# A constant matrix multiplied into an unread bank in TensorE's waits between routing and the first expert

## The chip, the cores and the metric

One NeuronCore of a Trainium2 chip runs the whole program. The metric is device time in microseconds (us) of one execution, lower is better. The time before is given as the median of three runs.

## What is computed

One decoder layer over 512 tokens of width 1024, all in float32. In the reference, cut to what matters here:

```python
h2 = rmsnorm(x, norm_ffn[i])
x = x + hierarchical_moe(h2, w_coarse[i], w_fine[i], w_expert_up[i], w_expert_down[i])

def hierarchical_moe(h, w_coarse, w_fine, w_up, w_down):
    coarse = jax.nn.softmax((t @ w_coarse).astype(f32), axis=-1)
    g_prob, g_idx = lax.top_k(coarse, 1)               # 1 of 4 groups
    ...
    top_vals, top_idx = lax.top_k(fine, TOP_K)         # 2 of its 4 experts
    top_w = jax.nn.softmax(top_vals, axis=-1) * g_prob
    ...
    gu = jnp.einsum('nd,edf->nef', t, w_up)
    act = jax.nn.silu(g_part) * u_part * gates[..., None].astype(t.dtype)
    out = jnp.einsum('nef,efd->nd', act, w_down)
```

Ahead of this stand a first RMSNorm, one input projection, a state-space branch and sliding-window attention side by side, gates that merge them, and an output projection that is added to x. There are 16 experts; each token goes to two of them.

## The kernel before

Every engine has its own program, written out by hand; semaphores tie them together. On each engine instructions run in the order written, so an instruction that waits holds up all behind it. Nothing plans the order: it is the text of the five blocks (`block.sync` for weight loads, `block.gpsimd` for gathers and scatters, `block.scalar`, `block.vector`, `block.tensor`).

Precision. Most large products take float32 operands that are split into a high part (rounded by a ScalarE copy into an fp32r tile) and a low part (VectorE subtracts the high part). TensorE then makes three fp32r products: high by high, high by low, low by high. So each weight piece costs ScalarE one pass and VectorE one pass before TensorE can use it. `product` (L1758 to L1764) does this for the first half of the kernel (lines L1761 to L1763), `up` (L2138 to L2140) for the experts' first matrix, `down_` (L2185 to L2192) for the second.

Beginning. TensorE waits for the tile of ones, which GpSimd writes (`ones_ready`, L610), and for the row of norm gains, which a DMA brings. Two matmuls (L1746) with one row of ones spread that row over 128 partitions in the banks `mb[0]` and `mb[1]`. VectorE multiplies the normalised rows by them (`scale_tile`, L1098). TensorE turns each tile of 128 tokens (`turn_tile`, L1755), ScalarE copies the high part (`turned_high`), VectorE takes the low part (L1152), and TensorE makes the keys and values of the tile (`keys_values`) into the banks `pj[0]` and `pj[1]` in turn. At the same time SyncE issues the loads of the first weight pieces and of many small parameters.

Output projection and routing. The output projection goes over eight units (two halves of the columns by four tiles of 128 tokens). Behind each unit TensorE turns its result (`turn_rows2`, L2010) and multiplies it by the router's weights (`router`, L2019) into `sc[0]`. When the last unit is done, the program goes on in this order:

1. VectorE ranks the logits in some fifteen small instructions and writes `chosen` (L1582).
2. TensorE multiplies `chosen` by a triangular matrix and by ones, to count the place of each token in its expert's list (L2075, L2078), and counts the tokens of each expert (L2081, into `mb[0]`).
3. VectorE writes `pos` (L1594) and, for each expert, a matrix `pick` that is one where a token has a given place (`pick_list`, L1603).
4. TensorE multiplies `pick` by the token numbers: `place_index` (L2090) for experts 0 and 1. VectorE makes them indices (L1624), and GpSimd's indirect DMA gathers the rows of that expert (L681) from `h2_rows` in memory, which `act.dma_start` (L973) has stored tile by tile.
5. VectorE computes each token's shares (L1628 to L1637) from an exponential that ScalarE makes (L1049), behind its two high parts of the first expert's weights (L982). TensorE places them (`place_shares`, L2098).
6. VectorE takes the low part of the first half of the first expert's weights (`low_up`, L1618) and the picks of experts 2 and 3.
7. TensorE turns the gathered rows (`turn_rows`, L2124), ScalarE and VectorE split them (`high_rows` L988, `low_rows` L1652, tile `xt_low`), and TensorE places lists 2 and 3 (`place_lists`, L2111).

Experts. For each expert e TensorE runs `up(e)` over eight slices of 128 (24 matmuls, waiting for each half of the weights, `up_low_done`, and of the rows, `xt_done`), the next two lists, the transposes of the activations of expert e-1 (`turn_act`), the transposes of the rows of expert e+1, and `down_(e-1)` into `mb[0]` and `mb[1]`. VectorE for expert e reads lists, makes two picks, takes the low parts of the two halves of expert e+1 (L1618) with the low part of a second matrix between them (L1672), of the activations (L1676) and of the rows (L1652), and then the product of gate and value (`swiglu`, L1658, L1660). Loads of weight halves go into a ring of 12 places, each released by `half_used` of TensorE.

Of the banks, `mb[1]` is last read before the output projection and next written by `down_(0)`; `pj[1]` is first written by the keys and values of the second tile. Each of these next writes starts an accumulation group anew.

The lines that set the order around the change:

```python
            pe.wait_ge(r_pe, 1)
            pe.wait_ge(const_ready, 8)
            pe.matmul(sc[0][:, 0:TT * NE], before[:], chosen[:].rearrange("p t e -> p (t e)"), start=True, stop=False)
...
            pe.wait_ge(route_done, 1)
...
            for e in range(2):
                place_index(e)
            place_shares()
            turn_rows(0)
            pe.wait_ge(idx_done, 1)
            place_lists(LISTS[1], LISTS[2])
            for e in range(NE - 1):
                up(e, range(DC))
```

Of the kernel before, what the change touches and what calls it, by code (L numbers as in the profile page):

```python
# [14 lines left out]
P = 128  # L15
# [9 lines left out]
def hybrid_layer(nc, x, norm_mix, w_in, lam_re, lam_im, log_dt, b_re, b_im, c_re, c_im, d_skip,  # L25
# [35 lines left out]
    with ExitStack() as ctx:  # L61
        def sb(name, shape, dt=F32):
            return ctx.enter_context(nc.sbuf_tensor(name, shape, dt))
# [121 lines left out]
        ones = sb("ones", [P, P], F32R)  # L185
# [51 lines left out]
        def bank(name):  # L237
            return ctx.enter_context(nc.psum_tensor(name, [P, 512], F32))

        pj = [bank("pj0"), bank("pj1")]  # L240
        tp = [bank("tp0"), bank("tp1")]
        sc_both, mb_both = (ctx.enter_context(nc.psum_tensor(name, [P, 2, 512], F32)) for name in ("sc_both", "m_both"))
        sc, mb = ([banks[:, b, :] for b in range(2)] for banks in (sc_both, mb_both))
# [134 lines left out]
        def out_bank(u, i):  # L378

            if u in BY_PIECE:  # L380
                return pj[i][:, 0:256]
            return pj[(u + 1) % 2][:, i * 256:(i + 1) * 256]

        def turned_bank(u, i):

            if u == BY_PIECE[1]:
                return tp[(u + i) % 2][:, 0:2 * P]
            return tp[u % 2][:, 2 * P * i:2 * P * (i + 1)]
# [47 lines left out]
        def expert(e):  # L436

            return e % NG * EPG + e // NG
# [20 lines left out]
        def piece_w(n, /, **dims):  # L459
            z = piece_size(n)  # L460
            pat = "p (%s) -> p %s" % (" ".join(dims), " ".join(dims))
            return [w[split_place(n)][:, 0:z].rearrange(pat, **dims) for w in (w_high, w_low)]
# [1272 lines left out]
        def _(pe):  # L1735
# [4 lines left out]
                return b  # L1740

            pe.wait_ge(ones_ready, 1)
            pe.wait_ge(mix_gain_loaded, 16)
            for f in range(2):
                pe.matmul(mb[f][:], ones[0:1, :].bitcast(F32), mix_gain[:, f * 512:(f + 1) * 512], start=True, stop=True  # L1746
                          ).then_inc(gain_full, 1)

            def turn_tile(t):
                for f in range(2):  # L1750
                    pe.wait_ge(xn_done, 2 * t + f + 1)
                    if t >= 2:
                        pe.wait_ge(h_low_done, 2 * (t - 2) + f + 1)
                    for k in range(4):
                        ins = pe.transpose(h_bank(t, f)[:, k * P:(k + 1) * P], xn[:, t, (4 * f + k) * P:(4 * f + k + 1) * P], ident[:])  # L1755
                    ins.then_inc(h_full, 1)

            def product(dst, terms, first=True, last=True):  # L1758

                for i, ((sh, sl), (mh, ml)) in enumerate(terms):  # L1760
                    pe.matmul(dst, sh, mh, start=first and i == 0, stop=False)  # L1761
                    pe.matmul(dst, sh, ml, start=False, stop=False)  # L1762
                    ins = pe.matmul(dst, sl, mh, start=False, stop=last and i == len(terms) - 1)  # L1763
                return ins  # L1764
# [235 lines left out]
            def turn_rows2(u, i):  # L2000

                hf, t = UNITS[u]
                pe.wait_ge(x2_done, 2 * u + i + 1)
                if u < 2:
                    pe.wait_ge(tp_free[u], (n_tp + 1 - u) // 2)
                else:
                    pe.wait_ge(h2T_done, 2 * u if u == BY_PIECE[1] and i else 2 * (u - 1))
                for k in range(2):
                    c0 = hf * 512 + (2 * i + k) * P
                    ins = pe.transpose(turned_bank(u, i)[:, k * P:(k + 1) * P], x2[:, t, c0:c0 + P], ident[:])  # L2010
                ins.then_inc(tp_full, 1)

            def router(u):

                hf, t = UNITS[u]
                for k in range(4):
                    if k % 2 == 0:
                        pe.wait_ge(h2T_done, 2 * u + k // 2 + 1)
                    ins = pe.matmul(sc[0][:, t * (NG + NE):(t + 1) * (NG + NE)], x2T[u % 2][:, k, :], rw[:, 4 * hf + k, :],  # L2019
                                    start=u == 0 and k == 0, stop=hf == 1 and k == 3, skip_group_check=True)  # L2020
                ins.then_inc(lg_full, 1)

            def out_piece(u, i, ks):

                hf, t = UNITS[u]
                w = piece_w(P_OUT + 2 * hf + i, k=DC, n=256)
                tok = slice(t * P, (t + 1) * P)
                for k in ks:
                    if u == 0:
                        pe.wait_ge(m_low_done, k + 1)  # L2030
                    ins = product(out_bank(u, i), [(both(m_hl, k, tok), both(w, k, slice(None)))], k == 0, k == DC - 1)
                return ins
# [34 lines left out]
            out_piece(u, 1, first_k)  # L2067
            turn_rows2(u, 0)
            out_piece(u, 1, last_k).then_inc(pj_full, 1)
            turn_rows2(u, 1)  # L2070
            router(u)

            pe.wait_ge(r_pe, 1)
            pe.wait_ge(const_ready, 8)
            pe.matmul(sc[0][:, 0:TT * NE], before[:], chosen[:].rearrange("p t e -> p (t e)"), start=True, stop=False)  # L2075
# [5 lines left out]
                ins = pe.matmul(mb[0][:, 0:NE], ones[:], chosen[:, t, :], start=t == 0, stop=t == TT - 1)  # L2081
            ins.then_inc(lg_full, 1)

            pe.wait_ge(route_done, 1)

            def place_index(e):

                pe.wait_ge(pick_done, e + 1)
                for t in range(TT):
                    ins = pe.matmul(sc[e][:, 128:130], pick[e][:, t, :], tg[:, expert(e), t, 0:2], start=t == 0, stop=t == TT - 1)  # L2090
                ins.then_inc(idx_full, 1)

            def place_shares():

                pe.wait_ge(shares_done, 1)
                for e in range(2):
                    for t in range(TT):
                        ins = pe.matmul(sc[0][:, 132 + 2 * e:134 + 2 * e], pick[e][:, t, :], tg[:, expert(e), t, 2:4], start=t == 0, stop=t == TT - 1)  # L2098
                ins.then_inc(idx_full, 1)

            def place_lists(lo, hi):
                for e in range(lo, hi):
                    place_list(e)

            def place_list(e):

                k = sum(e >= lo for lo in LISTS[1:])
                c0 = list_at(k) + 4 * (e - LISTS[k])
                pe.wait_ge(pick_done, e + 1)
                for t in range(TT):  # L2110
                    ins = pe.matmul(sc[0][:, c0:c0 + 4], pick[e % 2][:, t, :], tg[:, expert(e), t, :], start=t == 0, stop=t == TT - 1)  # L2111
                ins.then_inc(idx_full, 1)

            def row_chunk(rows, k):

                return rows.rearrange("r (a p b) -> r a b p", p=P, b=2)[:, k // 2, k % 2, :]

            def turn_rows(e):
                pe.wait_ge(gathered[e % 2], 16 * (e // 2 + 1))
                for f in range(2):  # L2120
                    if e:
                        pe.wait_ge(xt_done, e * 2 + (f - 1))
                    for k in range(4):
                        ins = pe.transpose(tp[f][:, k * P:(k + 1) * P], row_chunk(xg[e % 2], 4 * f + k), ident[:])  # L2124
                    ins.then_inc(xt_full, 1)
# [44 lines left out]
            def turn_act(e):  # L2170
                pe.wait_ge(act_done, (e + 1) * 2)
                if e:
                    pe.wait_ge(at_done, 2 * e)
                    pe.wait_ge(at_low_done, e)
                for k in range(2):
                    ins = pe.transpose(sc[1][:, k * P:(k + 1) * P], act_e[e % 2][:, k * P:(k + 1) * P], ident[:])
                ins.then_inc(at_full, 1)
# [29 lines left out]

            for e in range(2):
                place_index(e)
            place_shares()  # L2210
            turn_rows(0)
            pe.wait_ge(idx_done, 1)
            place_lists(LISTS[1], LISTS[2])
            for e in range(NE - 1):
                up(e, range(DC))
                if e < LAST_LISTS:
                    pe.wait_ge(idx_done, e + 2)
                    place_lists(LISTS[e + 2], LISTS[e + 3])
                if e:
                    turn_act(e - 1)  # L2220
                turn_rows(e + 1)
                if e:
                    down_(e - 1)
# [69 lines left out]
```

## Time and profile before

| what | value |
|---|---|
| median of three runs | 528.2 us (527.18 to 528.49) |
| the profiled execution: its own time | 527.75 us |
| the profiled execution: its span | 526.0 us |
| mean granted TensorE clock | 0.978 |
| TensorE (PE) busy | 502.1 us, 95% |
| VectorE (DVE) busy | 389.2 us, 74% |
| ScalarE (ACT) busy | 295.0 us, 56% |
| GpSimd (POOL) busy | 130.3 us, 25% |
| memory traffic | 94.21 MB, mean 179 GB/s |

The profile shows one execution, from its first to its last instruction (the span); the execution's own time is 1.75 us longer. Times are microseconds from the start of the span. "L2138" is line 2138 of the kernel. An instruction row names the engine, the line, the operation and "tile written <- tiles read"; in brackets stands the idle time of the engine before it, and what ended it. A row with "x8" merges eight instructions.
### The profile page before, as it was taken

Reading aid. Unit: us, or ns where it says so; the run is one execution under the profiler, and the core shown is the slowest. Engines: PE = TensorE matmul, PEld = TensorE weight load, DVE = VectorE, ACT = ScalarE, POOL = GpSimd, SP = SyncE. Lnnn points to the kernel's source line nnn. Section 1 sums busy time; section 2 is a strip of 40 time slices with the busy share of each in tenths; the row PEclk is TensorE's granted clock in tenths of the full one; section 3 lists DMA queues with packets and bytes.
Section 4 is the critical chain, followed back from the end, with each engine's and each line's share of the span. In section 5 each row is a group of like instructions: output and inputs, shape, how many; then the busy total and the mean of one; then the engine's idle time right before and its main releaser. Section 6 shows DMA issues by size and latency. Waiting matters only on the chain.

```text
span 526.0 us, 7338 instructions
## 1 busy us (share of the span) xinstructions
PE 502.1 (95%) x2634; PEld 408.9 (78%) x2634; DVE 389.2 (74%) x609; ACT 295.0 (56%) x522; POOL 130.3 (25%) x185
## 2 busy tenths in 40 slices
PE   6999999999999999999999999779999999999994
PEld 4888788787877887778888888767887777777773
DVE  4889876999898768765758423578988878878851
ACT  6634144767867777632335102344767778778751
POOL 1229429294570000000000000032223232222221
PEclk9999999999999999999999999858999999999999
DMA  8560562022112220244678547569999999987432
GB/s 312 73 224 1 126 196 80 1 81 80 31 51 80 62 61 0 61 120 121 186 274 295 226 190 290 189 228 412 376 331 332 327 341 349 314 298 201 144 54 45
DMA packets 62343, 94.21 MB, mean 179 GB/s; under 512 B 13952, under 2 KB 45728, under 8 KB 62306
## 3 DMA queue, kind: packets, MB, share of 16 engines
q1 hardware_dynamic: 56304, 80.84, 45.2%
q0 software_dynamic: 4752, 8.67, 6.9%
q10 hardware_dynamic: 1250, 4.22, 2.0%
q8 instruction: 22, 0.36, 0.3%
q14 instruction: 15, 0.12, 0.1%
HBM read 88.72 MB, written 12.58 MB: 193 GB/s over the span
## 4 chain that ended last, share of the span: by engine, by line
PE 78%; DVE 10%; SPq 4%; ACT 3%; DMA 2%; issue 2%; POOL 0%; DVEq 0%; POOLq 0%; ACTq 0%
PE pj L1761 10%; PE pj L1763 10%; PE pj L1762 10%; PE pj L2138 5%; PE pj L2140 5%; PE pj L2139 5%; PE m_both L2185 5%; PE tp L2124 3%; SPq L521 2%; DVE split L433 1%; PE m_both L2190 1%; PE m_both L2192 1%; PE m_both L2191 1%; PE m_both L1761 1%; PE sc_both L1762 1%
## 5 line engine op out<-in xcount | busy, mean ns | idle before, releaser
L1761 PE MATMUL pj<-h_high,split 128*128 128x512 f32 x192 | 76.7, 399 | 0.0
L1763 PE MATMUL pj<-h_high,split 128*128 128x512 f32 x192 | 74.9, 390 | 0.0
L1762 PE MATMUL pj<-h_low,split 128*128 128x512 f32 x192 | 74.8, 390 | 0.0
L1618 DVE TENSOR_TENSOR up_low<-arena_front,up_high 128x2048 fp32r<-128x2048 f32 x23 | 52.7, 2290 | 11.4 <-ACT up_high L982 11.3
L622 POOL TENSOR_TENSOR rstd<-ssq,half_col 128x1 f32<-128x1 f32 x8 | 4.4, 555 | 194.3 <-DVE ssq L1116 181.4
L982 ACT ACTIVATE up_high<-arena_front 128x2048 fp32r<-128x2048 f32 x23 | 44.2, 1927 | 10.8 <-PE pj L2140 9.7
L2138 PE MATMUL pj<-up_high,xt_high 128*128 128x512 f32 x120 | 48.0, 400 | 0.9 <-DVE xt_low L1652 0.9
L2140 PE MATMUL pj<-up_high,xt_low 128*128 128x512 f32 x120 | 47.7, 397 | 0.0
L2139 PE MATMUL pj<-up_low,xt_high 128*128 128x512 f32 x120 | 47.6, 397 | 0.0
L433 DVE TENSOR_TENSOR split<-arena_front,split 128x2048 fp32r<-128x2048 f32 (+1 forms) x20 | 42.7, 2136 | 5.1 <-ACT split L414 5.1
L414 ACT ACTIVATE split<-arena_front 128x2048 fp32r<-128x2048 f32 (+1 forms) x20 | 34.8, 1742 | 17.9 <-PE sc_both L1763 10.9
L1761 PEld LDWEIGHTS pj<-h_high,split 128*128 128x128 f32 x192 | 36.1, 188 | 9.6 <-issue 2.3
L1763 PEld LDWEIGHTS pj<-h_high,split 128*128 128x128 f32 x192 | 36.0, 188 | 7.8
L1762 PEld LDWEIGHTS pj<-h_low,split 128*128 128x128 f32 x192 | 36.1, 188 | 6.9
L689 POOL DMA_INDIRECT out_dram<-arena_back,idx_all x15 | 25.9, 1729 | 61.6 <-ACT arena_back L1013 53.5
L681 POOL DMA_INDIRECT arena_front<-h_rows,idx_all x16 | 20.1, 1255 | 68.8 <-PE tp L2124 56.7
L2185 PE MATMUL m_both<-arena_back 128*128 128x512 f32 x60 | 28.2, 593 | 0.0
L2138 PEld LDWEIGHTS pj<-up_high,xt_high 128*128 128x128 f32 x120 | 23.2, 194 | 6.0 <-DVE xt_low L1652 1.1
L2139 PEld LDWEIGHTS pj<-up_low,xt_high 128*128 128x128 f32 x120 | 23.2, 193 | 4.9
L2140 PEld LDWEIGHTS pj<-up_high,xt_low 128*128 128x128 f32 x120 | 23.1, 192 | 5.0
L1013 ACT ACTIVATE arena_back<-m_both,gate_all 128x512 f32<-128x512 f32 x30 | 19.0, 686 | 12.9 <-PE m_both L2192 12.9
L962 ACT ACTIVATE arena_back<-arena_back 128x512 f32<-128x512 f32 x8 | 5.0, 630 | 36.8 <-DVE arena_back L1139 36.8
(340 smaller groups left out, 1283.0 us busy)
## 6 DMA issues: line engine op xcount, KB each, us to landing
arena_front<-in_w_expert_up_dram SPq DMA_DIRECT2D x23, 1024.0 KB, 11.6
arena_back<-in_w_expert_down_dram SPq DMA_DIRECT2D x16, 1024.0 KB, 12.7
arena_front<-in_w_in_dram SPq DMA_DIRECT2D x12, 1024.0 KB, 5.3
arena_back<-in_w_expert_up_dram SPq DMA_DIRECT2D x9, 1024.0 KB, 13.4
arena_front<-in_w_out_dram SPq DMA_DIRECT2D x4, 1024.0 KB, 6.0
arena_back<-in_x_dram SPq DMA_DIRECT2D x4, 512.0 KB, 6.2
arena_front<-in_w_ssm_glu_gate_dram SPq DMA_DIRECT2D x8, 256.0 KB, 2.7
arena_front<-in_w_ssm_glu_val_dram SPq DMA_DIRECT2D x8, 256.0 KB, 3.2
```

The source lines that it names most:

```text
L414: nc.scalar.activation(w_high[split_place(n)][:, 0:z], raw[n % 2][:, 0:z], ACT.Copy).then_inc(high_done, 1)
L433: eng.tensor_tensor(w_low[s][:, 0:z], raw[n % 2][:, 0:z], w_high[s][:, 0:z].bitcast(F32), ALU.subtract).then_inc(low_done, 1)
L689: g.indirect_dma_start(out_rows, bass.IndirectOffsetOnAxis(idx_all[:, e:e + 1], 0), y_out[e % 2], None, compute_op=ALU.add, bounds_check=S ...
L982: act.activation(up_high[i % 3][:], ring[i % NH], ACT.Copy).then_inc(up_high_done, 1)
L1618: tt(up_low[i % NH][:], ring[i % NH], up_high[i % 3][:].bitcast(F32), ALU.subtract).then_inc(up_low_done, 1)
L1761: pe.matmul(dst, sh, mh, start=first and i == 0, stop=False)
L1762: pe.matmul(dst, sh, ml, start=False, stop=False)
L1763: ins = pe.matmul(dst, sl, mh, start=False, stop=last and i == len(terms) - 1)
L2138: pe.matmul(pj[e % 2][:], xs[0], ws[0], start=k == 0, stop=False)
L2139: pe.matmul(pj[e % 2][:], xs[0], ws[1], start=False, stop=False)
L2140: ins = pe.matmul(pj[e % 2][:], xs[1], ws[0], start=False, stop=k == DC - 1)
L2185: pe.matmul(y_bank(e, h), actT[e % 2][:, 1, :], down[e % 4][:, 1, cols[h]], start=True, stop=False)
```

## The change

A helper `spin(bank, n)` issues n matmuls with the tile of ones as both operands: 128 by 128 stationary, the same 128 columns four times (512 columns) moving, each starting and ending its own group in the bank that is given. It waits for nothing and signals nothing. It is called eight times, 38 matmuls in all: 3 before the wait for the gains and 2 behind the two gain matmuls (into `pj[1]`); 2 behind the last output product, 9 behind the last router product, 3 behind the counts, 11 behind the two indices, 7 behind the shares and 1 before the first expert (into `mb[1]`).

```diff
@@ -1740,11 +1740,19 @@
+            def spin(bank, n):
+
+                for _ in range(n):
+                    pe.matmul(bank[:].rearrange("p (k n) -> p k n", k=4), ones[:],
+                              ones[:].rearrange("p (k n) -> p k n", k=1).broadcast_to([P, 4, P]), start=True, stop=True)
+
             pe.wait_ge(ones_ready, 1)
+            spin(pj[1], 3)
             pe.wait_ge(mix_gain_loaded, 16)
             for f in range(2):
                 pe.matmul(mb[f][:], ones[0:1, :].bitcast(F32), mix_gain[:, f * 512:(f + 1) * 512], start=True, stop=True
                           ).then_inc(gain_full, 1)
+            spin(pj[1], 2)
@@ -2067,9 +2075,11 @@
             out_piece(u, 1, first_k)
             turn_rows2(u, 0)
             out_piece(u, 1, last_k).then_inc(pj_full, 1)
+            spin(mb[1], 2)
             turn_rows2(u, 1)
             router(u)
 
+            spin(mb[1], 9)
             pe.wait_ge(r_pe, 1)
@@ -2081,6 +2091,7 @@
                 ins = pe.matmul(mb[0][:, 0:NE], ones[:], chosen[:, t, :], start=t == 0, stop=t == TT - 1)
             ins.then_inc(lg_full, 1)
 
+            spin(mb[1], 3)
             pe.wait_ge(route_done, 1)
@@ -2207,10 +2218,13 @@
             for e in range(2):
                 place_index(e)
+            spin(mb[1], 11)
             place_shares()
+            spin(mb[1], 7)
             turn_rows(0)
             pe.wait_ge(idx_done, 1)
             place_lists(LISTS[1], LISTS[2])
+            spin(mb[1], 1)
             for e in range(NE - 1):
                 up(e, range(DC))
```

## Rows read from the trace of the kernel before

**Rows 1.** The page: span; TensorE's granted clock in 40 slices; chain by engine.
```profile
span 526.0 us, 7338 instructions
...
PEclk9999999999999999999999999858999999999999
...
PE 78%; DVE 10%; SPq 4%; ACT 3%; DMA 2%; issue 2%; POOL 0%; DVEq 0%; POOLq 0%; ACTq 0%
```

**Rows 2.** Stretches of 1 us: busy per engine (PE, PEld, DVE, ACT, POOL), PEclk, DMA.
```profile
339.00:340.00 1.00, 0.00 (x0) 0.00 (x0) 0.93 (x8) 1.00 (x1) 0.00 (x0) 0.56 1.00 414
...
359.00:360.00 1.00, 1.00 (x5) 0.81 (x4) 1.00 (x1) 0.30 (x1) 0.00 (x0) 0.70 1.03 426
```

**Rows 3.** Timeline of TensorE, last output product to first expert: start, length, what.
```profile
336.35 0.28 PE L1763 MATMUL pj<-split,m_low 128*128 128x256 f32 x1
337.14 0.44 PE L2010 MATMUL tp<-ident,arena_back 128*128 128x128 f32 x2 [0.52 <-DVE arena_back L1139]
...
338.20 0.62 PE L2019 MATMUL sc_both<-rw,arena_back 128*128 128x20 f32 x4 [0.26 <-DVE arena_back L1130]
340.97 0.42 PE L2075 MATMUL sc_both<-chosen,before 128*128 128x64 f32 x1 [2.14 <-DVE chosen L1582]
341.20 1.43 PE L2078 MATMUL sc_both<-chosen,ones 128*128 128x16 f32 x6
...
343.88 1.84 PE L2090 MATMUL sc_both<-tg,pick 128*128 128x2 f32 x8 [0.40 <-DVE pick L1603]
...
347.73 1.87 PE L2098 MATMUL sc_both<-tg,pick 128*128 128x2 f32 x8 [2.01 <-DVE tg L1637]
350.80 1.98 PE L2124 MATMUL tp<-ident,arena_front 128*128 128x128 f32 x8 [1.20 <-DMA arena_front<-h_rows,idx_all]
352.43 1.84 PE L2111 MATMUL sc_both<-tg,pick 128*128 128x4 f32 x8
354.14 0.77 PE L2138 MATMUL pj<-up_high,xt_high 128*128 128x512 f32 x1
```

**Rows 4.** The same timeline, first to third expert.
```profile
359.40 0.49 PE L2138 MATMUL pj<-up_high,xt_high 128*128 128x512 f32 x1
...
365.20 0.50 PE L2138 MATMUL pj<-up_high,xt_high 128*128 128x512 f32 x1 [0.93 <-DVE xt_low L1652]
...
370.79 0.95 PE L2111 MATMUL sc_both<-tg,pick 128*128 128x4 f32 x8
...
375.94 0.39 PE L2138 MATMUL pj<-up_high,xt_high 128*128 128x512 f32 x1
```

**Rows 5.** Timelines of ACT, POOL and DVE, 344 to 375 us.
```profile
344.79 0.25 ACT L1049 ACTIVATE arena_back<-arena_back 128x80 f32<-128x80 f32 x1
...
346.07 1.28 POOL L681 DMA_INDIRECT arena_front<-h_rows,idx_all  x1 [7.23 <-DVE idx_all L1624]
...
356.66 1.29 DVE L1603 TENSOR_TENSOR pick<-slot_no,pos 128x512 fp32r<-128x512 f32 x2
...
361.65 2.29 DVE L1618 TENSOR_TENSOR up_low<-arena_front,up_high 128x2048 fp32r<-128x2048 f32 x1 [1.50 <-ACT up_high L982]
364.46 1.29 DVE L1652 TENSOR_TENSOR xt_low<-tp,xt_high 128x512 fp32r<-128x512 f32 x2 [0.51 <-ACT xt_high L988]
...
373.53 1.28 DVE L1652 TENSOR_TENSOR xt_low<-tp,xt_high 128x512 fp32r<-128x512 f32 x2
```

**Rows 6.** The beginning: four of TensorE's timeline, one of the chain's pieces.
```profile
2.71 3.75 PE L1746 MATMUL m_both<-arena_back,ones 1*128 1x512 f32 x4 [2.71 <-DMA arena_back<-in_norm_mix_dram]
7.47 1.94 PE L1755 MATMUL tp<-ident,arena_back 128*128 128x128 f32 x8 [1.01 <-DVE arena_back L1098]
...
12.19 0.28 PE L1762 MATMUL pj<-split,h_high 128*128 128x256 f32 x1
...
13.39 0.28 PE L1763 MATMUL pj<-split,h_low 128*128 128x256 f32 x1
...
23.67 5.99 DMA arena_front<-in_w_in_dram
```

## The prediction

> **What bounds the kernel now.** The page comes first. TensorE is the chain for 78% of the span, and the row of its granted clock shows full speed everywhere except for a dent in the slices around 350 us [rows 1]. So I ask what TensorE does around that dent, and whether its time there sets the end. One-microsecond stretches show where the dent lies: in 339 to 340 the mean grant is 0.56, and in 359 to 360 it is 0.70 [rows 2]. If only the two levels 1.0 and 0.5 exist, the clock fell at about 339.1 us and rose at about 359.6 us. Between them lie about 20.5 us at 1.2 GHz instead of 2.4.
>
> The timeline of TensorE says why. The last output product starts at 336.35; after it come waits with short matmuls between them: 2.14 us for the chosen experts (DVE L1582), 2.01 us for the shares (L1637), 1.20 us for the gathered rows [rows 3]. From 354.14 the first expert's products run densely, and only at 359.40 do they step faster [rows 3, 4]. The price of half speed: twelve products took 354.14 to 359.40, 0.44 us each; twenty-four took 365.20 to 370.79, 0.233 us each. Eight small list matmuls took 1.84 us at half (352.43) and 0.95 us at full (370.79) [rows 3, 4], so each of this kind gets 0.11 us shorter.
>
> Then the other engines, since TensorE's gain counts only as far as they follow: the first gather starts at 346.07 after the index, ACT's exponential ends at 345.04, and after the first expert TensorE waits at 365.20 for DVE's xt_low [rows 4, 5]. Behind that, from 375.94, the timeline shows no idle time of TensorE before an expert's products [rows 4]; an expert earlier there should be an end earlier.
>
> **The spins themselves.** 38 matmuls of 512 columns, ones times ones, nobody reads them. At full clock each costs 0.233 us, at half 0.44. The question at each place is whether they end before what TensorE waits for, and whether they keep the clock up. I take both as yes and work it through; "after" times are on the scale of this execution.
> - Two behind the last output product: 336.35 plus about 0.12 plus 0.47 gives 336.95, before the transposes at 337.14 [rows 3]. Nothing lost.
> - Nine behind the router: it ends at 338.82; 9 x 0.233 = 2.1 gives 340.9, against 340.97 when the chosen experts come [rows 3]. Nothing lost, 0.1 us at most.
> - Positions: seven small matmuls. Before, 340.97 to the last one's end at 342.63 [rows 3]. At full clock seven save 0.11 each, 0.8 us. DVE's pos and picks follow 0.8 earlier, so the index matmuls start near 343.1 instead of 343.88. The four counts behind them and three spins (0.4 + 0.7) end near 342.9: hidden.
> - Index: eight matmuls from 343.88; the first four release the first gather. Four save 0.4. The gather starts 1.2 us earlier than 346.07, at about 344.9. It was on the chain, landing where the transposes start at 350.80, 4.7 us after its start [rows 3, 5]. I let it land 1.2 earlier, at 349.6; the bounds are 0 (another transfer holds it) and 1.2.
> - Eleven spins: from about 344.3 to 346.9. The shares cannot come much earlier than before, because DVE waits for the exponential that ACT finishes at 345.04 behind its own weight splits; that leaves 0.7 of 347.73, about 347.0 [rows 3, 5]. Hidden. The shares then take about 0.95 instead of 1.87 us, to 347.9, and seven spins (1.6) end at 349.5, just before the gathered rows. Hidden, but without margin.
> - Rows' transposes: 1.98 us at half [rows 3], 1.0 at full: 349.6 to 350.6. Lists to 351.4, one spin to 351.7. DVE's xt_low of the first half needs ACT's copy first; two such pieces take 1.29 us [rows 5], so it is ready at 351.6. The first expert starts at about 351.8 instead of 354.14: 2.4 us.
> - First expert: its first half (12 products, 2.8 us) ends at 354.6. The second half waits for up_low, which DVE begins after the second xt_low (352.3) and the lists' reads, at 352.5; at 2.29 us [rows 5] it is there at 354.8. So the products end at 357.7.
> - What is late next: **DVE**. From 354.8 it has two picks (1.29) and two up_low (2 x 2.29, less 0.1 for each overlap of two rows), to 360.5, then half of xt_low (0.65): 361.2 [rows 5]. TensorE has its lists (0.9) and transposes (about 1.0) behind it by 359.7, so it waits about 1.5 us, and the second expert starts at 361.2 instead of 365.20 [rows 4]: **4.0 us**. From there each engine goes at its old pace. TensorE took 10.7 us from 365.20 to the third expert at 375.94 [rows 4]; DVE took 9.1 us from xt_low at 364.46 to the next at 373.53 [rows 5]. So DVE reaches its next xt_low at 369.6 and TensorE its third expert at 371.9: TensorE is the bound again and the 4.0 us stay.
> - One step of each queue: SP, ACT and POOL get no new waits. The loads of later weights are released by TensorE's products, so they come earlier with it. Those behind the first gather (SP waits for it) start 1.2 us sooner. No cost.
>
> **The five at the beginning.** Three spins need 1.3 us at half clock; POOL writes the ones as its first own instruction, and TensorE sat idle to 2.71, when the gain row arrives; two lie between the gain's end at 6.46 and the transposes at 7.47, where at half clock they need 0.88 [rows 6]. The eight transposes there took 1.94 us, the half-clock size of the 1.98 in [rows 3], although the clock row of the page says 9 there [rows 1]; I go by the durations. By 12.19 the 256-column products step at 0.12 us (ten of them to 13.39) [rows 6], that is full speed. So the clock was up before the first product. Faster transposes would be hidden behind DVE and ACT, and the chain that ended last runs here through the queue's small loads and the w_in transfer at 23.67 [rows 6], not through TensorE. I take 0; bounds -0.7 (a run in which the clock rises later, half price of some products) and +0.1.
>
> The Trainium skill, "TensorE: Matmul & The Clock Gate", Part 4 (PE-mode transpose), says that transposes do not bring the full clock. The trace disagrees: between 7.47 and 12.0 there was nothing else, and at 12.19 it was full. By the page the kernel before would start its products at half and the five spins would have something to give; by the row they have nothing.
>
> **Sum.** 4.0 + 0 = 4.0 us off. The profiled execution took 527.75, its span is 526.0 [rows 1]; the median of the runs is 528.2, 0.45 above. 528.2 - 4.0 = **524.2**. With the gather held: transposes at 350.8, first expert at 352.9, its second half at 356.0 after up_low, DVE to the second expert at 362.3, which is 2.9 off, 525.3. With the start paying 0.7: 523.5. The likeliest case's own range is 523.2 to 525.5.
>
> **Rivals.**
> - *The clock dips between the nine and the eleven* (0.15). From 340.9 to 344.3 TensorE has 0.7 us of spins and otherwise small matmuls. If it falls there, the eleven run at 0.44: 4.8 us, to 349.1, past the shares; these and seven spins then end near 352 and the transposes slip 2.4 us. 524.2 + 2.4 = 526.6, and about 525.5 if the clock returns midway. For it: it fell once in such a stretch. Against: there was no dense work within it then.
> - *It falls at 339 as before and returns near 344* (0.06). The nine take 3.8 us and delay the positions by 1.4, the three add 0.9; the transposes start near 353.0 instead of 350.80. What full clock gives from there (about 3 us) is nearly all eaten: 527.6, no change.
> - **Slower: constant products do not raise the clock, or hold it** (0.06). Then nine cost 1.4 beyond their wait, three 0.9, eleven (4.8) end 2.6 past the shares, seven (3.1) end at about 357.4 where the transposes would have begun at 350.80, and one adds 0.4: about 7.0 late, 535.2. It decides from the point where the clock is still at half after 344. Against: the same shape of product, densely issued, raised it at 359.4; whether ones times ones counts alike no row shows.
> - *The start pays, too* (0.08): by the page's rule about transposes, or in runs where the rise comes late. Dense products at half cost as much again as at full; over the 5.3 us of 354.14 to 359.40 that was 2.5 us. The transfer chain at the start hides most; I give it 1.0: 523.2.
> - *Downstream swallows it* (0.03): transfers or DVE set the experts' pace, 527.5.
>
> **Chances.** The forecast has 0.62. About 0.3% (1.6 us) is what a measurement of this kernel can tell from no change. Faster: the forecast, the start, and most of the dip, 0.85. Same: the return near 344, downstream and the rest of the dip, 0.08. Slower: 0.07. The range takes the likeliest case's own and most of the dip: 522.8 to 526.8.
>
> **What would show it.** Right: a granted clock of 1.0 in every stretch from 336 to 362; the small matmuls near 0.10 us; the first gather about 1.2 us, the first expert 2.4 and the second 4 us earlier, with a wait for DVE between them; the start unchanged at 20 us. Wrong: a row of 0.5 over the eleven or seven spins, TensorE busy with spins when the shares or the gathered rows land, or a second expert earlier and the last one not.

## The result, and the profile after

The changed kernel takes 524.5 us (median of four, 523.72 to 524.65) against 528.35 (median of four, 527.18 to 528.87): ratio 0.9932, 95% interval 0.9913 to 0.9950, that is 3.6 us less, between 2.6 and 4.6. Forecast were 524.2 and a gain of 4.0. A second measurement on another chip gave 524.09 against 527.59, ratio 0.9935 (0.9917 to 0.9953).

The page of the profiled execution (its own time 524.46 us): span and clock row. They answer to [rows 1].
```profile
span 522.6 us, 7413 instructions
...
PEclk9999999999999999999999999989999999999998
```
In this stage the dent of the clock is down to one slice that reads 8, but it is not gone. (The last slice reads 8 too: there the clock is at half from 518.1 on, behind the last product, and that costs nothing. From the start of the third expert's products to the end of the span are 150.04 us here and 150.06 before.) Stretches of that stage (busy per engine, granted clock PEclk, DMA share, GB/s) say where it lies, and what TensorE did before it; compare [rows 2].
```profile
339.00:340.00 1.00, 1.00 (x6) 0.84 (x5) 0.97 (x7) 0.84 (x1) 0.00 (x0) 1.00 1.02 422
340.00:341.00 1.00, 0.99 (x7) 0.53 (x5) 0.90 (x5) 0.03 (x1) 0.00 (x0) 1.00 0.86 340
341.00:342.00 1.00, 1.00 (x12) 1.00 (x10) 0.56 (x3) 1.00 (x1) 0.00 (x0) 1.00 0.97 381
342.00:343.00 1.00, 0.99 (x5) 0.54 (x6) 0.97 (x3) 1.00 (x2) 0.00 (x0) 1.00 1.03 414
343.00:344.00 1.00, 1.00 (x9) 0.98 (x10) 0.52 (x2) 1.00 (x1) 0.00 (x0) 1.00 0.33 127
344.00:347.00 3.00, 3.00 (x9) 2.32 (x9) 2.08 (x10) 0.84 (x2) 1.97 (x2) 0.50 0.68 213
347.00:348.00 1.00, 1.00 (x5) 0.81 (x4) 1.00 (x1) 0.00 (x0) 0.31 (x1) 0.79 1.07 438
348.00:350.00 2.00, 2.00 (x15) 1.78 (x14) 1.80 (x3) 0.00 (x0) 0.00 (x0) 1.00 0.58 217
```
The clock holds at 339, where it fell before. It falls at 344.0, though TensorE had been busy for 0.99 us or more of every microsecond from 338 on, and is back at about 347.4. That is the first rival of the prediction. The timeline of TensorE (start, length, what, idle before) shows what it cost in this execution; L1746 is the spin, and the other rows answer to [rows 3, 4].
```profile
338.41 2.29 PE L1746 MATMUL m_both<-ones 128*128 128x512 f32 x9
340.70 0.30 PE L2085 MATMUL sc_both<-chosen,before 128*128 128x64 f32 x1
...
341.95 0.94 PE L1746 MATMUL m_both<-ones 128*128 128x512 f32 x3
342.91 1.11 PE L2101 MATMUL sc_both<-tg,pick 128*128 128x2 f32 x8
343.89 4.37 PE L1746 MATMUL m_both<-ones 128*128 128x512 f32 x11
348.09 0.95 PE L2109 MATMUL sc_both<-tg,pick 128*128 128x2 f32 x8
348.90 1.87 PE L1746 MATMUL m_both<-ones 128*128 128x512 f32 x7
350.60 1.11 PE L2135 MATMUL tp<-ident,arena_front 128*128 128x128 f32 x8
...
352.68 0.47 PE L2149 MATMUL pj<-up_high,xt_high 128*128 128x512 f32 x1
...
361.79 0.50 PE L2149 MATMUL pj<-up_high,xt_high 128*128 128x512 f32 x1 [1.25 <-DVE xt_low L1652]
...
372.56 0.39 PE L2149 MATMUL pj<-up_high,xt_high 128*128 128x512 f32 x1
```
The nine spins end where the chosen experts come. The eleven take 4.37 us in place of 2.8, so the shares are placed at 348.09, although VectorE had written them by 346.68. The rows of VectorE and GpSimd, against [rows 5]:
```profile
344.73 1.28 POOL L681 DMA_INDIRECT arena_front<-h_rows,idx_all  x1 [6.15 <-DVE idx_all L1624]
...
346.40 0.28 DVE L1637 TENSOR_TENSOR tg<-arena_back,tg 128x64 fp32r<-128x64 f32 x1
...
361.05 1.28 DVE L1652 TENSOR_TENSOR xt_low<-tp,xt_high 128x512 fp32r<-128x512 f32 x2
```
The first gather starts 1.34 us earlier (344.73 against 346.07), the first expert 1.5 (352.68 against 354.14). The second expert starts 3.4 us earlier (361.79 against 365.20), the third too (372.56 against 375.94), and so the span is shorter by 3.4 (526.0 to 522.6). From the second expert on nothing is won or lost.

### The profile page after: what moved, and what is told of

It reads as the page before. It is cut to its first block, busy times and chain, and to the rows that moved or that the text cites. A ratio compares the mean times of both kernels' runs of the same rounds, so it can differ in the third digit from the quotient of the medians.

```text
span 522.6 us, 7413 instructions
## 1 busy us (share of the span) xinstructions
PE 506.8 (97%) x2672; PEld 410.2 (78%) x2672; DVE 389.1 (74%) x609; ACT 294.9 (56%) x522; POOL 128.0 (24%) x185
## 4 chain that ended last, share of the span: by engine, by line
PE 77%; DVE 11%; SPq 4%; ACT 3%; issue 2%; DMA 1%; POOL 0%; DVEq 0%; POOLq 0%; ACTq 0%
PE pj L1769 10%; PE pj L1771 10%; PE pj L1770 10%; PE m_both L2196 5%; PE pj L2149 5%; PE pj L2150 5%; PE pj L2151 5%; PE tp L2135 3%; SPq L521 2%; PE m_both L1746 2%; DVE split L433 1%; PE m_both L2201 1%; PE m_both L2203 1%; PE m_both L2202 1%; DVE up_low L1618 1%
## 5 line engine op out<-in xcount | busy, mean ns | idle before, releaser
L681 POOL DMA_INDIRECT arena_front<-h_rows,idx_all x16 | 18.0, 1124 | 67.7 <-PE tp L2135 54.4
```

## The experiments

Twelve runs on three chips, four kernels on each. Every difference is to the kernel before on the same chip (527.8 us on the first, 527.6 on the two others) and comes from the ratio. Where an edit is to the calls of `spin`, it is a change of the kernel after, unless another kernel is named.

The mean granted clock of an execution is used below. It says how long the clock's record is at half, not where. (The record reads full before the first rise, where the durations show half.) Behind the last product each profile has 1.3 to 4.5 us of half clock that cost nothing. A mean of 0.993 or less needs 6.8 us or more at half, so at least 2 us of it lie elsewhere; a mean of 0.997 or more leaves less elsewhere than the shortest dip that a profile shows (3.4 us); at 0.995 or 0.996 a short dip can hide.

### Which spins carry the gain

Only the five at the beginning:
```diff
-            spin(mb[1], 2)
-            spin(mb[1], 9)
-            spin(mb[1], 3)
-            spin(mb[1], 11)
-            spin(mb[1], 7)
-            spin(mb[1], 1)
```

> Only the five spins at the beginning. My theory: they give nothing, since the transposes they speed up are hidden; 528.3 us against 528.3 of before, within 0.3, with the same fall of the clock at about 339. Rival (the start pays too, with an early clock at the first keys and values): 0.3 to 1.0 less, about 527.6.

Measured: 527.08 us, ratio 0.9988 (0.9975 to 1.0002), 0.6 less with an interval that just holds zero. The spins did not bring an early clock. In this execution the products of the keys stepped at 0.21 us until 15.8; the timeline of TensorE:
```profile
7.42 1.94 PE L1763 MATMUL tp<-ident,arena_back 128*128 128x128 f32 x8
...
12.43 0.55 PE L1769 MATMUL pj<-split,h_high 128*128 128x256 f32 x1 [0.98 <-DVE h_low L1152]
...
15.55 0.41 PE L1771 MATMUL pj<-split,h_low 128*128 128x256 f32 x1
...
357.00:358.00 1.00, 1.00 (x5) 0.78 (x5) 1.00 (x3) 0.00 (x0) 0.54 (x1) 0.83 1.02 410
...
364.11 0.50 PE L2146 MATMUL pj<-up_high,xt_high 128*128 128x512 f32 x1 [0.93 <-DVE xt_low L1652]
```
That late rise cost little: the transposes behind the last output product start at 337.30, against 337.14 before. What made this execution's span 1.1 us shorter than that of before (524.9 against 526.0) lies elsewhere. The clock fell at 340.3 and was back at 357.3 (339.1 and 359.6 before), so the second expert starts at 364.11 in place of 365.20, which is all of the 1.1. Eleven of the twelve executions have a mean clock of 0.980 or more, ten of the 35 of before. So the 0.6 us are no sign of a gain at the beginning; why the dip was shorter, no run shows.

Only the 33 between routing and first expert (the first two calls removed):
```diff
-            spin(pj[1], 3)
-            spin(pj[1], 2)
```

> Only the 33 spins between routing and first expert. My theory: all of the gain is here, 524.5 us (3.8 less than before). Rival (the start pays part): 525.0 to 525.5, and the start-only kernel has the rest.

Measured: 525.08 us, ratio 0.9960 (0.9940 to 0.9980), 2.1 less (1.1 to 3.2). I had expected all of the gain, 3.8. It holds most of it; the rest is not told apart from zero. Its executions scatter from 523.4 to 528.2, and three of twelve have a mean clock of 0.992 or less.

Only the 2, 9 and 3:
```diff
-            spin(pj[1], 3)
-            spin(pj[1], 2)
-            spin(mb[1], 11)
-            spin(mb[1], 7)
-            spin(mb[1], 1)
```

> Only the 2, 9 and 3 spins. My theory: the clock stays full to about 344, so the positions and the index are 1.2 us earlier and with them the gather; then TensorE has waits again and the clock falls before the first expert, whose products start at half. The second expert starts about 1.2 us earlier than before: 527.1 us. Rival (the clock does not fall any more once it is kept past the ranking): 525.

Measured: 527.15 us, ratio 0.9991 (0.9975 to 1.0007), 0.5 less, not told apart from zero. Stretches of this kernel, same columns as above:
```profile
342.00:344.00 2.00, 1.99 (x12) 1.47 (x12) 1.50 (x4) 2.00 (x2) 0.00 (x0) 1.00 0.67 266
344.00:345.00 1.00, 0.03 (x1) 0.00 (x0) 0.30 (x3) 0.82 (x2) 0.30 (x1) 0.53 0.61 74
...
353.00:357.00 4.00, 4.00 (x12) 3.23 (x12) 3.82 (x6) 1.36 (x1) 2.29 (x1) 0.50 1.02 418
357.00:358.00 1.00, 1.00 (x5) 0.77 (x4) 1.00 (x2) 0.00 (x0) 0.00 (x0) 0.64 1.03 426
```
The clock holds past 339 and falls at 344, and the first expert's products run at half until 357.7. A fall that is only put off is worth little.

Only the 11, 7 and 1:
```diff
-            spin(pj[1], 3)
-            spin(pj[1], 2)
-            spin(mb[1], 2)
-            spin(mb[1], 9)
-            spin(mb[1], 3)
```

> Only the 11, 7 and 1 spins. The clock falls at 339 as before; the eleven start near 345.7 at half and raise it before the first expert. My theory: the eleven hold up the shares by 1 to 2 us, but transposes, lists and the whole first expert run at full clock: 525.8 us, 2.5 less than before. Rival (spins started at half clock only get in the way): 529 or more.

Measured: 526.32 us, ratio 0.9985 (0.9965 to 1.0006), 0.8 less by the ratio and 1.5 by the medians; executions from 525.6 to 529.8. In the profiled one (525.64 us) the clock fell at 341.9 and was back at 348.7, under the eleven:
```profile
341.00:342.00 1.00, 1.00 (x9) 1.00 (x10) 0.52 (x4) 0.76 (x1) 0.00 (x0) 0.94 1.01 406
```
Up to there this kernel is the one of before, whose clock fell at 339.1: the same instructions, and a fall 2.8 us later. So that the clock holds past 339 in one profile says little; the comparison is between all of them. In this stage it fell at 339.1, 340.3 and 341.9 in the three profiles without the nine spins, and in the ten with them (512 columns wide) never before 343.7.

The first expert ran at full clock, but the shares were placed at 349.23. So neither half of the routing spins gives its share alone: the first without the last hands the fall on, the last without the first pays for the return.

### What the spins cost where they stand in the way

22 in place of 11, 14 in place of 7:
```diff
-            spin(mb[1], 11)
+            spin(mb[1], 22)
             place_shares()
-            spin(mb[1], 7)
+            spin(mb[1], 14)
```

> All spins, but 22 in place of 11 and 14 in place of 7. My theory: spins past the wait stand on the path; at full clock the shares come 2.5 us later, the seven more add 1.6, and the transposes start near 353.5 in place of 350.6. 3 us slower than the change, about 0.8 less than before. Rival (unread products cost nothing, they overlap): as the change, 3.8 less than before.

Measured: 526.98 us, ratio 0.9990 (0.9979 to 1.0001), 0.5 less than before; the spread kernel below, on the same chip, has 524.47. TensorE:
```profile
344.06 5.28 PE L1746 MATMUL m_both<-ones 128*128 128x512 f32 x22
349.18 0.95 PE L2109 MATMUL sc_both<-tg,pick 128*128 128x2 f32 x8
349.99 3.49 PE L1746 MATMUL m_both<-ones 128*128 128x512 f32 x14
353.31 1.11 PE L2135 MATMUL tp<-ident,arena_front 128*128 128x128 f32 x8
```
At full clock (0.23 us each), with no dip in this profile and a mean clock of 0.995 or more in all twelve executions, the transposes start 2.7 us later than in the profile of the change. An unread product costs its whole time once the wait it fills is over: eleven more are 2.6 us, and the shares are placed at 349.18, against 346.46 in the profile of the changed VectorE order below, which has no dip here either and runs 0.3 us earlier.

8, 4 and none in place of 11, 7 and 1:
```diff
-            spin(mb[1], 11)
+            spin(mb[1], 8)
             place_shares()
-            spin(mb[1], 7)
+            spin(mb[1], 4)
...
-            spin(mb[1], 1)
```

> All spins, but 8 in place of 11, 4 in place of 7, none in place of 1. In the profile of the change the clock fell at 344.0 for 3.4 us, the eleven took 4.4 us and the shares, ready near 346.7, were placed at 348.09. My theory: the eleven and seven are in the way only when that dip comes. With 8 and 4 the shares come up to 1.2 us and the transposes up to 0.9 us earlier in such a run, and nothing changes in the others: 4.0 us less than before, 0 to 0.5 better than the change. Rival (the last spins are what brings or keeps the clock): it falls in the wait for the gathered rows and the gain shrinks to 2.5 or less.

Measured: 525.95 us, ratio 0.9982 (0.9963 to 1.0001), 0.9 less. My theory fell. In the profile the shares and the transposes did come earlier (347.12 and 349.75), but the clock fell a second time, in the second expert:
```profile
348.00:361.00 13.00, 11.23 (x63) 9.12 (x62) 12.10 (x17) 6.85 (x8) 2.74 (x2) 1.00 0.89 346
361.00:362.00 1.00, 0.95 (x3) 0.77 (x4) 0.97 (x3) 1.00 (x1) 0.54 (x1) 0.63 1.03 406
362.00:364.00 2.00, 2.00 (x6) 1.58 (x5) 2.00 (x6) 1.17 (x2) 0.00 (x0) 0.50 1.02 408
```
It fell at 361.3, 0.2 us after the second expert's products began; before them TensorE had its lists and transposes and then waited 1.3 us for VectorE. The change has the same wait there, and its clock did not fall. Eleven of the twelve executions have a mean clock of 0.992 or less. I did not take apart which of the three cuts did this.

### The dip, and the width of the spins

The spins spread into the stretch of small matmuls:
```diff
-            for t in range(TT):
-                ins = pe.matmul(mb[0][:, 0:NE], ones[:], chosen[:, t, :], start=t == 0, stop=t == TT - 1)
-            ins.then_inc(lg_full, 1)
-
-            spin(mb[1], 3)
+            spin(mb[1], 5)
             pe.wait_ge(route_done, 1)
...
-            for e in range(2):
-                place_index(e)
-            spin(mb[1], 11)
+            place_index(0)
+            spin(mb[1], 2)
+            place_index(1)
+            for t in range(TT):
+                ins = pe.matmul(mb[0][:, 0:NE], ones[:], chosen[:, t, :], start=t == 0, stop=t == TT - 1)
+            ins.then_inc(lg_full, 1)
+            spin(mb[1], 8)
```

> The change with wide matmuls spread into the stretch of small ones after which the clock fell at 344: 5 in place of 3, 2 between the two indices, the four counts moved behind the indices, 8 in place of 11. My theory: the fall came from the stretch of small matmuls with only three spins in it; with seven there it comes in fewer runs or none (mean granted clock 0.996 or more), worth 0.95 us at the transposes where it came: 4.2 less than before. Rival (the fall has to do with the waits, not with the width of the matmuls): clocks of 0.992 as often as with the routing-only kernel, 3.8 less.

Measured: 524.47 us (six executions, 523.30 to 524.72), ratio 0.9939 (0.9923 to 0.9954), 3.2 less; 4.2 were expected. Stretches, then TensorE of the profiled execution, whose span is 521.5 us:
```profile
343.00:344.00 1.00, 1.00 (x9) 0.91 (x8) 0.20 (x2) 1.00 (x1) 0.00 (x0) 1.00 0.07 25
344.00:347.00 3.00, 3.00 (x19) 2.41 (x18) 2.42 (x10) 0.50 (x2) 2.29 (x2) 1.00 0.86 269
...
349.34 1.23 PE L2131 MATMUL tp<-ident,arena_front 128*128 128x128 f32 x8 [0.18 <-DMA arena_front<-h_rows,idx_all]
...
351.53 0.47 PE L2145 MATMUL pj<-up_high,xt_high 128*128 128x512 f32 x1
...
360.64 0.50 PE L2145 MATMUL pj<-up_high,xt_high 128*128 128x512 f32 x1 [1.24 <-DVE xt_low L1652]
```
Here the whole stage ran at full clock, and every time of the prediction's main case can be held against it (below). TensorE's wait at the transposes is for the gathered rows again, 0.18 us.

The same kernel on the third chip, beside the change:

> The spread kernel again (5 in place of 3, 2 between the indices, counts behind them, 8 in place of 11). My theory: clock 0.996 or more in every execution, all within about 1.5 us of each other, 0.3 to 1.0 less than the change. Rival (the dip costs nothing): as the change.

Measured: 524.75 us (seven executions, 523.85 to 526.51), ratio 0.9949 (0.9932 to 0.9967), 2.7 less. I had expected it 0.3 to 1.0 below the change beside it, and every mean clock at 0.996 or more; three of the seven have 0.995.

> The change once more, beside the others on one chip. My theory: 3.4 to 3.8 us less than before; its executions fall into two kinds, with a mean clock of 0.996 or more (no dip) and of 0.994 or less (a dip near 344), the second 0.5 to 2 us longer. Rival (the dip costs nothing): both kinds alike.

Measured: 524.09 us (eight executions), ratio 0.9935, 3.4 less. Mean clocks and times are of two kinds. Five executions have 0.997 or more and take 523.28 to 524.17, on average 523.9. Three have 0.989 to 0.992 and take 525.18, 526.65 and 527.71, on average 526.5. The difference is 2.6 us on this chip, more than the 0.5 to 2 expected. In the first measurement two executions with 0.992 and 0.993 took 524.46 and 524.65, on average 0.4 more than the two with 0.996 and 0.997. So the price goes from next to nothing to all of the gain, and five of the twelve executions measured of this kernel have 0.993 or less. Only the two profiled ones show where their half clock lies. The one on this chip is the longest of the twelve:
```profile
344.00:347.00 3.00, 3.00 (x9) 2.52 (x10) 1.98 (x10) 0.94 (x2) 1.74 (x2) 0.50 0.61 208
...
350.00:354.00 4.00, 4.00 (x13) 3.22 (x13) 1.59 (x5) 0.00 (x0) 0.00 (x0) 0.51 0.84 283
...
344.39 5.04 PE L1746 MATMUL m_both<-ones 128*128 128x512 f32 x11
349.23 1.70 PE L2109 MATMUL sc_both<-tg,pick 128*128 128x2 f32 x8
350.79 3.30 PE L1746 MATMUL m_both<-ones 128*128 128x512 f32 x7
353.92 1.11 PE L2135 MATMUL tp<-ident,arena_front 128*128 128x128 f32 x8
```
The clock was at half from 343.7 to 353.9. The transposes start at 353.92 in place of the 350.80 of before, the second expert at 365.10 in place of 365.20: nothing is won in this execution. The spread kernel had no such execution in thirteen (lowest mean clock 0.995), and none in eight more without its start spins. So the long dips are gone; short ones may hide in the eight of these 21 that have 0.995 or 0.996 and no profile; the three profiles show none near 344. That the spread spins are what removed them is not shown: the kernel with 22 and 14 has the change's own stretch of small matmuls, and none of its twelve executions is below 0.995 either. Of the seven profiles with that stretch behind nine wide spins five have a fall between 343.7 and 344.6, and two (22 and 14, VectorE's order) have none. Nor is it shown that the spread kernel is faster. Its median is 0.7 us above the change's on this chip, and the two are equal over both (0.9939 and 0.9949 against 0.9932 and 0.9935).

Part of its time on the third chip is the beginning. Its profile there:
```profile
9.48 1.31 PE L1763 MATMUL sc_both<-ident,arena_back 128*128 128x128 f32 x8
...
13.32 0.55 PE L1769 MATMUL pj<-split,h_high 128*128 128x256 f32 x1 [2.53 <-DVE h_low L1152]
...
13.00:14.00 1.00, 0.68 (x3) 0.71 (x4) 1.00 (x2) 1.00 (x3) 0.00 (x0) 0.55 0.98 173
```
The clock rose under the transposes from 9.48 (1.31 us in place of 1.97), TensorE then waited 2.53 us for the keys' operands, and the clock fell again at 13.1, 0.2 us before the first of the products. Most of that wait is not the spins' doing: ScalarE began to split the first weights at 9.43, when their load was in, in place of 7.97 in the profile of the change. There the same fast transposes left a wait of 1.17 us, and the clock held. The transposes behind the last output product came at 338.18, 1.0 us later than in [rows 3].

The spread kernel without the start spins:
```diff
-            spin(pj[1], 3)
...
-            spin(pj[1], 2)
```

> The spread kernel without the five spins at the beginning; the narrow scatter of that kernel should show less than the start-only kernel could (0.6 less than before, interval -1.3 to +0.1). My first theory (the beginning gives nothing): as the spread kernel within 0.2. Rival (the start pays, since in some executions the first keys and values run at half clock): 0.4 to 0.8 us longer, with the longer ones having lower mean clock.

Measured: 525.47 us (524.43 to 526.59), ratio 0.9957 (0.9941 to 0.9973), 2.3 less. The spread kernel with them has 0.9949 on this chip; the 0.4 us between them lies well inside both intervals. The profiles say more. At the first products of the keys the clock was at full in four of the eight profiles with the five wide spins at the beginning, and in three of the five without. Nothing shows that the spins there bring it earlier.

Each spin as two matmuls of 16 columns in place of one of 512:
```diff
-                for _ in range(n):
-                    pe.matmul(bank[:].rearrange("p (k n) -> p k n", k=4), ones[:],
-                              ones[:].rearrange("p (k n) -> p k n", k=1).broadcast_to([P, 4, P]), start=True, stop=True)
+                for _ in range(2 * n):
+                    pe.matmul(bank[:, 0:16], ones[:], ones[:, 0:16], start=True, stop=True)
```

> The change with each spin made two matmuls of 16 columns in place of one of 512, at the same places. My theory: the chip holds the clock for wide streams, not for instructions; the narrow ones take about the same time (0.2 us a pair) and the clock falls near 339 as before and returns only in the first expert; 528 us, no change against before, or up to 2 us slower where they get in the way at half clock. Rival (any instruction stream without waits holds it): as the change, 3.8 less.

Measured: 533.58 us, ratio 1.0120 (1.0096 to 1.0144), 6.3 more than before. Stretches and TensorE:
```profile
339.00:340.00 1.00, 1.00 (x10) 1.00 (x9) 0.68 (x6) 0.46 (x1) 0.42 (x1) 0.88 0.99 389
350.00:354.00 4.00, 4.00 (x21) 4.00 (x20) 2.29 (x2) 0.00 (x0) 3.10 (x1) 0.50 0.31 81
...
357.36 1.98 PE L2134 MATMUL tp<-ident,arena_front 128*128 128x128 f32 x8
```
TensorE was busy in every microsecond from 339 to 371, and the clock fell at 339.8 all the same and stayed at half until 367. This kernel and the change differ in the width of the spins alone, so what held the clock in the other kernels is the wide streams, not that instructions run. The mechanism was as expected; I had its price too low, at up to 2 us.

### VectorE's order

```diff
+            low_up(0, 1)
             low_rows(0)
             read_lists(1)
-            low_up(0, 1)
```

> The change, and VectorE takes the low part of the second half of the first expert's weights (L1618) before that of the gathered rows, in which time it sat idle for 1.21 us. My theory: VectorE bounds the second expert's start (TensorE waits 1.25 us there); the first expert starts up to 1 us later but the second 0.5 to 1.0 earlier: 0.5 to 1.0 us better than the change, 4.5 less than before. Rival (where the clock does not dip VectorE has no such idle time, and the swap only delays the first expert): no change against the change or 0.5 worse.

Measured: 526.48 us, ratio 0.9973 (0.9958 to 0.9989), 1.4 less than before, so worse than the change. The rival was right, and more than right:
```profile
352.00:353.00 1.00, 0.01 (x1) 0.02 (x1) 1.00 (x3) 1.00 (x1) 0.00 (x0) 1.00 1.07 434
353.00:354.00 1.00, 1.00 (x3) 0.86 (x4) 1.00 (x4) 0.24 (x1) 0.00 (x0) 0.65 1.00 406
```
The swap gives TensorE a new wait of 1.06 us before the first expert, and the clock falls at 353.3, and again at 363.5. The second expert starts at 363.14, later than the 361.79 of the change. How much of the loss is the order and how much the clock, the run does not separate.

## Why the prediction was right, and where not

**The size.** 4.0 us were forecast; five executions without a dip give 527.6 - 523.9 = 3.7, all executions together 3.6 on one chip and 3.4 on another. The range and the sign held.

**The chain of small times.** The first profile of the spread kernel, which kept its clock, stands for the prediction's main case (it is the fastest of its six executions, and its routing begins some 0.6 us earlier than that of before, the transposes behind the last output product at 336.56 against 337.14), so 0.6 is taken off each forecast here. Transposes of the gathered rows: 349.0 forecast, 349.34 measured. First expert: 351.2 and 351.53. Its second half: 354.2 and 354.52. Second expert: 360.6 and 360.64, with a wait for VectorE of 1.5 forecast and 1.24 measured. So the terms up to the first expert were 0.3 us too good, and the term that decides, the second expert's start, held to 0.1: VectorE, which sets it, was done with its low parts at 359.98, against 359.9 forecast. The span of that execution, 521.5, is 4.5 below that of before, and 3.9 without the 0.6. The 0.3 lies in the gather. It started at 344.37 (344.3 forecast), but its rows let the transposes start 4.97 us later, not 4.7. In the profile of the change the transposes were held by spins, not by it.

**The step that did not hold** is the assumption under every row of the sum: that TensorE at full clock in the gaps keeps full clock throughout. I had called the stretch from 340.9 to 344 the weak place, and gave it 0.15. It is there in both profiles of the change, and five of twelve executions have the low mean clock that goes with it. Its price was forecast at 1.3 to 2.4 us; measured are 0.4 on one chip (two executions against two) and 2.6 on another (three against five). I had argued against it that before there had been no dense work in the stretch where the clock fell; I counted the three spins as enough. In part it is luck that the forecast of the median held: most executions have no dip, and the two of the first measurement that point to one lost only 0.4 us by it.

**The slower rival** (the spins do not hold the clock, 535.2 us) did not come. Ones times ones hold and raise the clock: with the nine it never fell before 343.7, without them by 341.9 at the latest, and it came back under the eleven at 347.4 (change) and 348.7 (last nineteen). The narrow kernel realises its mechanism, unread matmuls that do not hold the clock and stand in the way, and at 533.6 us its price of 7.0 was right within 0.7.

**DVE as what is late next** held: the wait of 1.24 to 1.25 us before the second expert is there in each profile with a fast first expert.

**The beginning.** I took 0, and gave 0.08 to a gain of 1.0. Measured are 0.6 and 0.4 us, neither clear of zero, and in the profile of the first the gain is a shorter dip at 340 us. So nothing shows a gain, and a small one is not excluded. My reason was incomplete all the same: I argued from one execution in which the clock was up before the first key product. In others it was not (15.8 with start spins alone, and two of the five profiles without start spins), or rose and fell again. What held is that a late rise is absorbed later: the start-only execution ran its first products at half and reached the end of the output projection 0.16 us later than before. The Trainium skill's rule on transposes ("TensorE: Matmul & The Clock Gate", Part 4) is that they do not bring the full clock. The traces go both ways: in the spread kernel's run above eight transposes from 9.48 took 1.31 us against 1.94 from 7.43, so the clock rose there, behind two spins and transposes, and in the last-nineteen kernel, without start spins, it rose under them too (1.72 us in place of 1.97). In the start-only kernel it came only at 15.8, under the dense products.

The Trainium skill, on the same page in "Why this matters for your kernels", ties drops of the clock to idle gaps between matmuls. The traces agree in part: a wait stood before the fall at 353.3 (VectorE's order swapped, 1.06 us), but the change waits 1.25 us before its second expert and its clock held. They disagree at 344.0 in the change, where TensorE had been busy since 338, and with the half clock of the narrow kernel, which stayed for 27 us under a TensorE that was busy throughout.

## What to carry to other kernels

Filling TensorE's waits pays when the clock would fall in them, dense work follows, and the fillers end before the wait does: here 3.7 us, and all but 0.5 of it gone with 18 fillers too many. Look for wide streams, not for busy time, when asking what holds the clock: small matmuls back to back did not hold it in the narrow kernel, and may be what lost it at 344. Read the mean clock of every execution beside the profile of one, since the same kernel had a dip in some and none in others; but the mean does not say where the half clock lies. Judge such a change over a dozen executions.

## What was not expected

- A busy TensorE and a clock that falls, or stays low: at 344.0 in the change, behind six microseconds with 0.99 us or more of work in each, and for 27 us (339.8 to 367) in the narrow kernel.
- A fall just after dense work has begun: at 353.3, 0.3 us after the first expert's products began (swapped order), and at 361.3, 0.2 us after the second expert's (8 and 4 spins). Both follow a wait (1.06 and 1.26 us) that was over.
- The same instructions, and a fall at 339.1 in one execution and at 341.9 in another.
- The return differs between executions of one kernel: in the change 3.4 us after the fall in one profile, and 10.2 in another, with dense spins in most of that time.
- A clock that rose under the first transposes and fell again before the first products, in an execution whose first weights came late.
